# Low parts of streamed weights written over their raw loads, and one unit more of lead

## What is computed

```python
for l in range(DEPTH):                                    # blocks 0 and 1
    h = rms_norm(x, attn_norm[l])
    x = x + hybrid_mixer(h, w_in[l], ...)
    h = rms_norm(x, mlp_norm[l])
    x = x + squared_relu_mlp(h, w_up[l], w_down[l])
x = rms_norm(x, final_norm)
...                                                       # blocks 2 and 3
u = rms_norm_2(h, g_mix_pre)
(gq, gk, gv, gg, ra_f, ra_b, aq, ak, av, gate_a, gate_b) = jnp.split(u @ w_in, offsets, axis=-1)
```

## Time and profile before

| | |
|---|---|
| median of three runs | 2021.16 us |
| profiled execution | 2020.3 us, span 2018.5 us |
| PE busy | 1929.1 us, 96% of the span |
| DVE busy | 1243.2 us, 62% |
| ACT busy | 999.4 us, 50% |
| POOL busy | 127.9 us, 6% |
| mean granted TensorE clock | 0.978 of full speed |
| DMA queue of SP | 311.87 MB, 49.8% of 16 engines' time |

### The profile page before, as it was taken

One profiled execution on the slowest core, in us unless ns is written; L12 is line 12 of the kernel. 1 busy time (PEld: TensorE's weight loads), 2 busy tenths in 40 slices (PEclk: granted clock), 3 DMA queues, 4 the chain that ended last, 5 costly groups with the idle time before them and its releaser, 6 DMA issues.

```text
span 2018.5 us, 24878 instructions
## 1 busy us (share of the span) xinstructions
PE 1929.1 (96%) x9125; PEld 1571.2 (78%) x9125; DVE 1243.2 (62%) x2041; ACT 999.4 (50%) x1510; POOL 127.9 (6%) x52
## 2 busy tenths in 40 slices
PE   7999999999999999999999999999889999999996
PEld 6777888888777788887777787888677778878885
DVE  6756673547746574556569566665565784666645
ACT  5445554444445554444643745454446356454543
POOL 0000008300000008300000000000000000000000
PEclk9999999999999999999999999999979999999998
DMA  6444555556443555554534444646444343445562
GB/s 226 131 134 115 169 181 176 184 185 186 132 124 114 182 173 177 186 183 137 181 127 118 130 149 146 198 147 218 140 122 142 120 142 129 158 156 181 175 199 72
DMA packets 167327, 315.18 MB, mean 156 GB/s; under 512 B 12180, under 2 KB 20070, under 8 KB 167080
## 3 DMA queue, kind: packets, MB, share of 16 engines
q1 hardware_dynamic: 166612, 311.87, 49.8%
q10 hardware_dynamic: 596, 1.73, 0.2%
HBM read 312.51 MB, written 1.05 MB: 155 GB/s over the span
## 4 chain that ended last, share of the span: by engine, by line
PE 88%; DVE 6%; ACT 3%; issue 2%; DMA 0%; ACTq 0%; DVEq 0%
PE acc L541 76%; PE mix L513 4%; PE mix L569 2%; PE mix L550 1%; DVE lo L1268 1%; PE mix L774 1%; PE mix L699 1%; PE mix L745 1%; DVE x L1351 1%; PE mix L764 1%; ACT junk L992 1%; ACT hi L948 1%; PE mix L732 0%; PE mix L557 0%; DVE kT L1286 0%
## 5 line engine op out<-in xcount | busy, mean ns | idle before, releaser
L948 ACT ACTIVATE hi<-raw 128x1024 fp32r<-128x1024 f32 x600 | 634.5, 1061 | 635.1 <-PE acc L541 586.7
L1268 DVE TENSOR_TENSOR lo<-raw,hi 128x1024 fp32r<-128x1024 f32 x552 | 666.3, 1226 | 244.4 <-ACT hi L948 229.2
L541 PE MATMUL acc<-hi,xTh 128*128 128x512 f32 (+3 forms) x1760 | 700.0, 398 | 16.5 <-DVE lo L1268 6.7
L541 PE MATMUL acc<-hi,xTl 128*128 128x512 f32 (+3 forms) x1760 | 683.9, 389 | 0.0
L541 PE MATMUL acc<-lo,xTh 128*128 128x512 f32 (+3 forms) x1760 | 683.2, 388 | 0.0
L541 PEld LDWEIGHTS acc<-hi,xTh 128*128 128x128 f32 x1760 | 338.1, 192 | 94.4 <-issue 26.8
L541 PEld LDWEIGHTS acc<-hi,xTl 128*128 128x128 f32 x1760 | 337.1, 192 | 67.7
L541 PEld LDWEIGHTS acc<-lo,xTh 128*128 128x128 f32 x1760 | 338.4, 192 | 61.2
L921 POOL TENSOR_TENSOR lo<-raw,hi 128x1024 fp32r<-128x1024 f32 x48 | 127.7, 2688 | 698.9 <-ACT hi L948 698.9
L541 PE MATMUL acc<-hi,hTh 128*128 128x512 f32 x432 | 171.8, 398 | 0.0
L541 PE MATMUL acc<-hi,hTl 128*128 128x512 f32 x432 | 171.2, 396 | 0.0
(11 more groups left out here) (209 smaller groups left out, 1644.0 us busy)
## 6 DMA issues: line engine op xcount, KB each, us to landing
raw<-in_w_in SPq DMA_DIRECT2D x200, 512.0 KB, 3.7
raw<-in_w_ffn_in SPq DMA_DIRECT2D x80, 512.0 KB, 4.1
raw<-in_w_mlp_up SPq DMA_DIRECT2D x64, 512.0 KB, 3.9
raw<-in_w_mlp_down SPq DMA_DIRECT2D x64, 512.0 KB, 4.5
raw<-in_w_ffn_out SPq DMA_DIRECT2D x44, 512.0 KB, 4.5
raw<-in_w_out SPq DMA_DIRECT2D x32, 512.0 KB, 4.2
raw<-in_w_o_gla SPq DMA_DIRECT2D x16, 512.0 KB, 3.8
raw<-in_w_o_attn SPq DMA_DIRECT2D x16, 512.0 KB, 3.8
```

Of the source, the lines that this page charges most:

```text
L541: last = nc.tensor.matmul(out, a[:, t * P:(t + 1) * P], w[:, slot, part, 0:c.n], start=(k == 0 and a is ah and w is L.hi), stop=(k == c.k_ ...
L948: nc.scalar.activation(L.hi[:, slot], L.raw[:, slot], ACT.Copy).then_inc(*n.up("hi_ready"))
L1268: v.tensor_tensor(L.lo[:, slot], L.raw[:, slot], L.hi[:, slot].bitcast(F32), ALU.subtract).then_inc(*n.up("low_by_dve"))
```

## The change

Low parts are written over the raw loads: `raw` and `lo` become two names for the same memory, a ring of seven slots. `hi` gets a ring of its own with five. Therefore the load of unit u now waits until PE has used unit u-7. The high part of u waits until PE has used u-5. `HALVES_AHEAD` goes from 3 to 4 and `LOWS_AHEAD` from 2 to 3; ACT makes the high part of unit 3, and DVE the low part of unit 2, before the stream begins. High and low parts are made over the columns and row tiles that the unit has (`part`), so the memset and its semaphore go.

```diff
-RING = 4
+RING = 7
+HI_RING = 5
...
+    def part(self, u):
+
+        c = self.unit[u][0]
+        return slice(0, min(2, c.k_tiles)), slice(0, c.n)
...
-        raw = sb("raw", [P, RING, 2, COLS])
-        hi = sb("hi", [P, RING, 2, COLS], F32R)
-        lo = sb("lo", [P, RING, 2, COLS], F32R)
+        hi = sb("hi", [P, HI_RING, 2, COLS], F32R)
...
+        ring = arena - RING * 2 * COLS * 4
+        raw = nc.alloc_sbuf_tensor_at("raw", [P, RING, 2, COLS], F32, offset=ring)
+        lo = nc.alloc_sbuf_tensor_at("lo", [P, RING, 2, COLS], F32R, offset=ring)
...
+                wh = L.hi[:, u % HI_RING, part, 0:c.n]
+                wl = L.lo[:, u % RING, part, 0:c.n]
+                for a, w in ((ah, wh), (ah, wl), (al, wh)):
...
         if u >= RING:
-            sp.wait_ge(*n.at(*L.plan.low[u - RING]))
+            sp.wait_ge(*n.at("unit_used", u - RING + 1))
...
-LOWS_AHEAD = 2
+LOWS_AHEAD = 3
...
-HALVES_AHEAD = 3
+HALVES_AHEAD = 4
...
-        if u >= RING:
-            act.wait_ge(*n.at("unit_used", u - RING + 1))
-        nc.scalar.activation(L.hi[:, slot], L.raw[:, slot], ACT.Copy).then_inc(*n.up("hi_ready"))
+        if u >= HI_RING:
+            act.wait_ge(*n.at("unit_used", u - HI_RING + 1))
+        nc.scalar.activation(L.hi[:, u % HI_RING, *L.plan.part(u)], L.raw[:, slot, *L.plan.part(u)], ACT.Copy).then_inc(*n.up("hi_ready"))
...
-    act.wait_ge(L.sems["ring_clear"], 1)
     high(0)
...
     high(2)
+    high(3)
...
-            v.tensor_tensor(L.lo[:, slot], L.raw[:, slot], L.hi[:, slot].bitcast(F32), ALU.subtract).then_inc(*n.up("low_by_dve"))
+            v.tensor_tensor(L.lo[:, slot, *L.plan.part(u)], L.raw[:, slot, *L.plan.part(u)], L.hi[:, u % HI_RING, *L.plan.part(u)].bitcast(F32), ALU.subtract).then_inc(*n.up("low_by_dve"))
...
-    v.memset(L.raw[:, 0:2, :, MQ:], 0.0).then_inc(L.sems["ring_clear"], 1)
...
     tell("x_rows", 2 * NT)
+    low(2)
```

More of the change, by code:

```diff
@@ L175 @@
 SIGNALS = {
+    'raw4_loaded'         : [86, 0, 0],
+    'raw5_loaded'         : [85, 0, 0],
+    'raw6_loaded'         : [85, 0, 0],
     'unit_used'           : [600, 0, 0],
     'hi_ready'            : [600, 0, 0],
[L178 to L181, removed]
+    'raw0_loaded'         : [86, 0, 0],
+    'raw1_loaded'         : [86, 0, 0],
+    'raw2_loaded'         : [86, 0, 0],
+    'raw3_loaded'         : [86, 0, 0],
     'bank0_filled'        : [103, 0, 0],
@@ L244, in __init__ @@
         self.n = len(self.unit)
-        assert self.n % RING == 0
         self.chunks, uses = [], [0, 0]
@@ L312, in up @@
         return self.sems[name], count
-ONCE = ["x0_loaded", "x1_loaded", "ident_loaded", "const_loaded", "ring_clear", "stored", "gain_rows_loaded", "gain_cols_ready"]
+ONCE = ["x0_loaded", "x1_loaded", "ident_loaded", "const_loaded", "stored", "gain_rows_loaded", "gain_cols_ready"]
 EVAC, TURN = 1, 3
@@ L393, in build @@
         arena = big - 30 * 1024
-        assert nc.sbuf_base <= arena and spare + 10240 <= nc.sbuf_usable_end, (nc.sbuf_base, arena)
+        ring = arena - RING * 2 * COLS * 4
+        raw = nc.alloc_sbuf_tensor_at("raw", [P, RING, 2, COLS], F32, offset=ring)
+        lo = nc.alloc_sbuf_tensor_at("lo", [P, RING, 2, COLS], F32R, offset=ring)
+        assert nc.sbuf_base <= ring and spare + 10240 <= nc.sbuf_usable_end, (nc.sbuf_base, arena)
         def at(name, kib, shape, dt=F32, base=arena):
@@ L525, in unit @@
         c, j = L.plan.unit[u]
-        slot = u % RING
         if u == c.first and c.turn:
@@ L539, in unit @@
                 out = L.acc[:, 2 * c.pair + t, 0:c.n]
-                for a, w in ((ah, L.hi), (ah, L.lo), (al, L.hi)):
-                    last = nc.tensor.matmul(out, a[:, t * P:(t + 1) * P], w[:, slot, part, 0:c.n],
-                                            start=(k == 0 and a is ah and w is L.hi),
+                wh = L.hi[:, u % HI_RING, part, 0:c.n]
+                wl = L.lo[:, u % RING, part, 0:c.n]
+                for a, w in ((ah, wh), (ah, wl), (al, wh)):
+                    last = nc.tensor.matmul(out, a[:, t * P:(t + 1) * P], w,
+                                            start=(k == 0 and a is ah and w is wh),
                                             stop=(k == c.k_tiles - 1 and a is al))
@@ L920, in gpsimd_program @@
             pool.wait_ge(*n.at("hi_ready", u + 1))
-            nc.gpsimd.tensor_tensor(L.lo[:, slot], L.raw[:, slot], L.hi[:, slot].bitcast(F32), ALU.subtract).then_inc(*n.up("low_by_pool"))
-LOWS_AHEAD = 2
+            nc.gpsimd.tensor_tensor(L.lo[:, slot, *L.plan.part(u)], L.raw[:, slot, *L.plan.part(u)], L.hi[:, u % HI_RING, *L.plan.part(u)].bitcast(F32), ALU.subtract).then_inc(*n.up("low_by_pool"))
+LOWS_AHEAD = 3
 def gain_col(L, tag, gain, k):
```

## The result

The changed kernel takes 2026.8 us (median of 12 runs, 2022.65 to 2028.58), the kernel before 2021.57 us in the same comparison (12 runs, 2020.75 to 2022.84). The ratio is 1.0023, with a 95% interval of 1.0015 to 1.0032: 0.23% slower, where I had forecast 0.36% faster. The prediction was wrong. The profiled execution took 2027.09 us with a span of 2025.3, 6.8 us more than the span before; the mean granted clock is 0.977, as before (0.978).

What follows compares the result with a forecast made beforehand. PE was taken to bound the kernel (88% of the chain), with only its gaps to win. Terms 3.3 + 1.9 + 2.1 = 7.3 us took the profiled 2020.3 to 2013.0, a median of 2013.9 us; range 2009 to 2019.

Steps and rivals of the forecast that it cites:

- Low over raw: DVE's subtraction writing over its own input takes as long as with a separate output, 424 against 425 ns: nothing.
- Opening of the third block: Transposes of x to those of the decay columns: late low parts no longer stop PE, 3.3 us won, bound below 1.3.
- First GLU chunk: Third and fourth blocks: PE's stop for a part and a later eviction wait go, 1.9 us together, bounds 1.4 and 2.0.
- Unlisted gaps: Small PE gaps in 256-wide last GLU chunks and at the first two blocks' sigmoid gates: 2.1 us won, bound below 0.7.
- Linear attention: Two 2.0 us low-part waits go, but PE waits as long for DVE at head transposes: nothing, bound above 4.0.
- Loads: Loads get two units of time, some land late, but PE isn't stopped: nothing, bound 7.2 us of loss.
- start: Extra high parts at kernel start delay the first norm about 2 us, before PE needs it: nothing, bound 2 us loss.
- A: Lateness of DVE or ACT comes back elsewhere; only the third block's opening stays won: 2017.9 us, chance 0.12.
- B: The two long attention waits are won too, 4.0 us more: 2009.9 us, chance 0.10.
- D: The change does nothing because every gap is replaced by another: 2021.2 us, chance 0.06.
- S: Late loads make ACT wait, with evictions behind it, 12 us lost against 7.3 won: 2025.9 us, chance 0.08.
- C: The moved attention wait brings the low clock, 1.7 us lost each time, 3.4 in both blocks: 2017.3 us, chance 0.12.

Runs made afterwards that it cites:

- on 128 bytes: Kernel before or changed kernel with upper SBUF buffers rounded to multiples of 128 bytes instead of 32: 2009.52 us before, 1998.43 us changed.
- the ring alone: Changed kernel with upper buffers at multiples of 128 bytes, but the ring of raw loads and low parts moved down 32 bytes: 2024.51 us, ratio 1.0015 to the kernel before.

## Why the prediction was wrong, point by point

- **The pace, and what it costs PE to find the low parts in the ring: the step that failed.** "Matmuls of 512 columns start 0.23 us apart, so a unit of 12 takes 2.72 us" was read in one stage and taken for all stages and both kernels. The trace of before had two paces, 2.72 with xT and 2.81 with hT, and its cause would have priced the change. "Low over raw ... Nothing" asked what the new place of the low parts costs DVE, and was right there: 1223 ns for a low part after, on 128 bytes, 1226 before. PE reads them too, and I didn't ask about PE. The term at nothing was the one mis-sized: off 128 bytes, the ring alone costs 26 us against the version with everything on 128 (2024.51 against 1998.43). The whole loss of the changed kernel against that version is 28.4 us, and one rounding takes it away.
- **Opening of the third block, 3.3 us.** Right in size where the address is held still. In the changed kernel on 128 bytes it takes 955.42 - 924.14 = 31.28 us (timeline of PE, first fence), against the forecast 31.29 and the 34.63 before. In the changed kernel itself it takes 33.21, at the slower pace and with a granted clock of 0.85 (second fence: stretch, us, busy time of PE, PEld, DVE, ACT and POOL, clock, DMA share, GB/s); before, the clock was 0.90 over this stretch.

```profile
924.14 1.04 PE L522 MATMUL mix<-const,x 128*128 128x128 f32 x8
...
955.42 0.60 PE L693 MATMUL mix<-const,proj 128*16 128x128 f32 x4
```

```profile
938.20:971.41 33.21, 33.21 (x153) 28.40 (x152) 25.40 (x64) 12.18 (x20) 0.00 (x0) 0.85 0.45 130
```

- **First GLU chunk, 1.9 us.** The stopped unit became 0.75 and 0.78 us shorter in the two blocks, 1.5 together. Part of the 0.4 us for the eviction was seen in the changed kernel alone (0.43).
- **Unlisted gaps, 2.1 us.** Right: 0.36 + 0.30 in each last GLU chunk, 0.37 and 0.35 at the gates, 2.04 in all.
- **Linear attention, nothing.** Right: on 128 bytes, PE starts 2.0 us sooner behind the first place and 1.9 later at the second, in both blocks; in the changed kernel itself the second takes back only 1.6.
- **"So every engine keeps its order and its work, and each part is ready one unit, 2.72 us, earlier against PE."** The order is kept, but not what an engine finds released. I took the lead for the main cause, with the narrow parts as a help. By the profiled spans on 128 bytes (2006.4, 2003.6, 2002.4, 1998.9 us) the narrow parts bring 2.8 us, the seven load slots 1.2 and the lead with its slot 3.5. Most of the opening's gain comes with the narrow parts alone (35.06 to 31.98, then 31.28 us). And I didn't see that the new slot, left free, would have won as much before the norms. So the sum was nearly right for partly wrong reasons, which is luck in that part.
- **Loads, nothing; start, nothing.** Right for seven slots, and near an edge: one slot fewer costs 12 us. The first unit ends 0.2 us later.
- **Rivals.** A, B and D didn't occur. S exists at six slots. C occurred elsewhere: in the first two blocks, not behind the moved wait. Behind PE's wait of 1.83 us for DVE before 72.69 the changed kernel's granted clock falls to 0.50, the lower of the two levels (1.2 and 2.4 GHz), for 3.41 us; before, it stayed at 1.00 behind the same wait. It costs 1.6 us in each of the two blocks.

```profile
72.69 0.89 PE L560 MATMUL mix<-kT,qT 96*128 96x256 f32 x4 [1.83 <-DVE kT L1296]
```

```profile
74.17:77.58 3.41, 3.41 (x10) 2.63 (x9) 2.44 (x5) 1.93 (x5) 0.00 (x0) 0.50 0.00 0
```

What stays open: between the two kernels on 128 bytes the medians differ by 11.1 us and the profiled spans by 7.5, with terms that add up to about 7.6. Runs of each of the two differ by 2 to 3 us, and the stretches at the lower clock level fall in other places in each trace; I can't tell which of the two has the remaining 3 us. Why the pace depends on the start wasn't tried either, nor any other type than fp32r.

## What to carry to other kernels

When a change moves a buffer, work out the start address of every operand that PE reads, before and after, and compare the pace by operand in the trace; here a mean of 400 ns in place of 395 was all that PE's groups showed of it. Try a ring one slot deeper than the lead needs: here a part whose slot was freed by the unit just finished stood in front of the work that the end of a chunk released, and the free slot won as much as a unit of lead. Give lead where an engine was seen to be late, and look at what it is put in front of elsewhere.

## What the runs showed of the hardware

An fp32r matmul of 128x128 by 128x512 starts every 226 to 227 ns when its operands start on multiples of 128 bytes of the partition, and every 229 to 237 (medians by kind of product) when the ring that the moving operand comes from, the stationary operand or both start 32 bytes short of one. With both 64 bytes off the mean was 230 to 238, by kind of product. Moving the upper buffers down by 96 bytes was worth 1.4% of the changed kernel, more than twice the 0.5% that the change gains where the address is held still.
